# Issuing the gate matrices' stores from ScalarE's queue, one batch behind their eviction, instead of from the sync engine's queue

## The reference, cut to what matters

```python
def peer(xn, w_q, sub_keys, u_tab, v_tab):
    q = (xt @ w_q).reshape(T, PEER_HEADS, 2, PEER_HALF)
    s = jnp.einsum('thpc,hpnc->thpn', q, sub_keys)
    s_top, i_top = lax.top_k(s, PEER_TOPK)
    cand_s = s_top[:, :, 0, :, None] + s_top[:, :, 1, None, :]
    cand_i = i_top[:, :, 0, :, None] * N_KEYS + i_top[:, :, 1, None, :]
    best_s, pos = lax.top_k(cand_s.reshape(...), PEER_TOPK)
    gate = jax.nn.softmax(best_s)
    ...
        act = gelu(jnp.einsum('tkd,td->tk', u_tab[ib], xb))
        return jnp.einsum('tk,tkd->td', act * gb, v_tab[ib])
```

## Time and profile before

| | us |
|---|---|
| median of 3 runs | 1511.92 |
| lowest and highest run | 1506.97 and 1512.82 |
| the profiled execution, its time | 1506.98 |
| its span in the trace | 1505.2 |
| TensorE, VectorE, ScalarE, GpSimd busy over the span | 1447.5, 1245.2, 828.0, 506.6 |
| mean granted TensorE clock, share of full speed | 0.99 |

### The profile page before, as it was taken

How to read it: one execution, slowest core, us unless ns; L and a number is a source line. 1 busy time by engine, 2 the same in 40 slices (tenths; PEclk the granted TensorE clock), 3 DMA queues, 4 the chain that set the end, 5 groups by cost and what they waited for, 6 DMA issues and landing times.

```text
span 1505.2 us, 25263 instructions
## 1 busy us (share of the span) xinstructions
PE 1447.5 (96%) x9438; PEld 1307.3 (87%) x9438; DVE 1245.2 (83%) x2383; ACT 828.0 (55%) x1571; POOL 506.6 (34%) x425
## 2 busy tenths in 40 slices
PE   6999789999999999999989989999999999999999
PEld 6898678779999999999989879999888888878787
DVE  4638778674799799899669849999999989998997
ACT  4453454133244677778768644444566555555653
POOL 4111530010078877777621103323222212221210
PEclk9999899999999999999999999999999999999999
DMA  5230001421158799999899999998999999999993
GB/s 190 89 102 1 8 30 34 166 98 71 51 194 276 272 334 351 360 346 333 301 375 392 394 334 356 392 376 325 398 410 411 412 408 410 411 408 411 403 405 133
DMA packets 168871, 420.49 MB, mean 279 GB/s; under 512 B 12944, under 2 KB 100144, under 8 KB 152240
## 3 DMA queue, kind: packets, MB, share of 16 engines
q1 hardware_dynamic: 126064, 234.06, 42.8%
q0 software_dynamic: 27712, 167.82, 28.3%
q10 hardware_dynamic: 14976, 17.05, 3.1%
HBM read 372.44 MB, written 46.40 MB: 278 GB/s over the span
## 4 chain that ended last, share of the span: by engine, by line
PE 41%; DMA 15%; DVE 12%; issue 4%; ACT 2%; POOL 1%; SPq 0%; ACTq 0%; DVEq 0%
DMA v_raw<-in_peer_v 9%; PE bank L2105 6%; PE bank L2100 6%; PE bank L2101 6%; DMA gates<-gate_stage 4%; PE bank L2122 4%; PE bank L2431 3%; PE bank L2433 3%; PE bank L2432 3%; DVE v_lo L2507 3%; PE bank L2419 2%; PE bank L2420 2%; PE bank L2421 2%; DVE v_lo_late L2507 2%; DVE pair_sum L1822 1%
## 5 line engine op out<-in xcount | busy, mean ns | idle before, releaser
L2100 PE MATMUL bank<-x_hi,u_split 128*128 128x320 f32 x832 | 252.9, 316 | 3.6 <-ACT u_split L2160 3.6
L2101 PE MATMUL bank<-x_lo,u_split 128*128 128x320 f32 x832 | 246.4, 309 | 0.0
L1798 POOL DMA_INDIRECT scores<-in_peer_uv,pair_index x86 | 106.5, 1239 | 379.5 <-DVE pair_sum L1822 375.4
L2478 ACT ACTIVATE act_tile<-onehots 128x384 f32<-128x384 f32 x128 | 124.2, 970 | 74.2 <-DVE act_lo L2520 71.5
L2100 PEld LDWEIGHTS bank<-x_hi,u_split 128*128 128x128 f32 x832 | 157.1, 189 | 4.6 <-issue 4.6
L2101 PEld LDWEIGHTS bank<-x_lo,u_split 128*128 128x128 f32 x832 | 156.8, 188 | 0.0
L2105 PE MATMUL bank<-x_hi,u_split 128*128 128x320 f32 x832 | 139.6, 309 | 0.7 <-POOL u_split L2003 0.7
L2003 POOL TENSOR_TENSOR u_split<-u_raw,u_split 128x1024 fp32r<-128x1024 f32 x41 | 99.4, 2426 | 91.5 <-DVE u_split L2003 58.2
L2105 PEld LDWEIGHTS bank<-x_hi,u_split 128*128 128x128 f32 x832 | 127.1, 189 | 0.9 <-POOL u_split L2003 0.9
L2431 PE MATMUL bank<-v_hi,act_hi 128*128 128x512 f32 x304 | 120.0, 395 | 3.0 <-DVE v_lo L2507 2.9
L2433 PE MATMUL bank<-v_hi,act_lo 128*128 128x512 f32 x304 | 119.1, 392 | 0.0
(11 more groups left out here) (434 smaller groups left out, 4022.2 us busy)
## 6 DMA issues: line engine op xcount, KB each, us to landing
v_raw<-in_peer_v SPq DMA_DIRECT2D x128, 512.0 KB, 11.2
u_raw<-in_peer_u SPq DMA_DIRECT2D x64, 512.0 KB, 5.6
u_raw_more<-in_peer_u SPq DMA_DIRECT2D x64, 512.0 KB, 5.8
gates<-gate_stage SPq DMA_DIRECT2D x24, 1024.0 KB, 13.4
onehots<-gates SPq DMA_DIRECT2D x32, 768.0 KB, 11.9
early_gelus<-early_gelu ACTq DMA_DIRECT2D x104, 160.0 KB, 5.5
gelu_tile<-early_gelus SPq DMA_DIRECT2D x104, 160.0 KB, 11.2
w_raw<-in_w_in SPq DMA_DIRECT2D x9, 1024.0 KB, 5.0
```

The source lines that it names most:

```text
L1798: pool.indirect_dma_start(self.slot(k), None, self.table, bass.IndirectOffsetOnAxis(ap=self.sidx[:, k:k + 1], axis=0)).then_inc(self.lande ...
L2100: nc.tensor.matmul(out, uh[:, q, w], m.xh[:, k, P + NS:], start=(k == 0), stop=False)
L2101: nc.tensor.matmul(out, uh[:, q, w], m.xl[:, k, P + NS:], start=False, stop=False)
L2478: nc.scalar.activation(af[n % 2][:], gt[:, it % 2, :, jj], ACT.Copy).then_inc(gate_cols, 1)
```

## The change

`store_gates` moves from SP's program into ScalarE's. ScalarE calls it in every odd turn n from 3 on, right behind `evict(n - 1, 0)`, for batch n - 2, whose second eviction was made in the turn before; the last store (batch 47) comes behind the loop. What is stored, its size, its pieces, the two halves of `stage` and the semaphores stay as they were. In the changed kernel ScalarE's lines stand about ten lower in number (L2150 for 2160, L2163 for 2173, L2182 for L2192), and the store is L2191.

```diff
@@ SP
-                def store_gates(n):
-                    b, k = BATCHES[n]
-                    q = n // 2 % 2
-                    banks.wait_taken(sp, ("G", b, k, BT // 4 - 1))
-                    t0 = (b - 1) * P + (k + 1) * BT - ST
-                    sp.dma_start(gates[:, :, t0:t0 + ST, :].rearrange("g i t j -> i g (t j)"),
-                                 stage[:, q].rearrange("p g t j -> p g (t j)")).then_inc(stored[q], 16)
...
                 for n in range(NB_):
                     for t in ups_of[n + AHEAD_U] if n + AHEAD_U < NB_ else []:
                         load_u(t + NU)
-                    if n % 2:
-                        store_gates(n)
@@ ScalarE
+                def store_gates(n):
+                    b, k = BATCHES[n]
+                    q = n // 2 % 2
+                    banks.wait_taken(act, ("G", b, k, BT // 4 - 1))
+                    t0 = (b - 1) * P + (k + 1) * BT - ST
+                    act.dma_start(gates[:, :, t0:t0 + ST, :].rearrange("g i t j -> i g (t j)"),
+                                 stage[:, q].rearrange("p g t j -> p g (t j)")).then_inc(stored[q], 16)
...
                             for t in ups_of[n - 1][i:i + 1]:
                                 gelu(t)
                             evict(n - 1, i)
+                            if i == 0 and n >= 2 and n % 2 == 1:
+                                store_gates(n - 2)
...
                     if n == LAST_DOT + 1:
                         up_rows.gelu(act)
+                store_gates(NB_ - 1)
                 for n in range(EARLY - LAST, EARLY):
                     gelu(n)
```

## The result

| | before | after |
|---|---|---|
| median, us | 1511.08 | 1531.88 |
| lowest and highest of four runs | 1506.97 and 1512.82 | 1527.6 and 1534.04 |
| the profiled execution, its time | 1506.98 | 1533.86 |
| its span | 1505.2 | 1532.0 |

The ratio is 1.0132, with a 95% interval from 1.0114 to 1.015: the change costs 20.8 us. The forecast was 1515 us, 3 us slower, with a range to 1525. The sign is right and the size isn't.

What follows compares the result with a forecast made beforehand. TensorE bounds routing until 758 us, then ScalarE's waits for stores of gates show one for one. Loop +7, burst -2, end -2 make +3 on the 1511.9 median: 1515 us, 8 in 10 between 1505 and 1525.

Steps and rivals of the forecast that it cites:

- The loop of the late part: Six pairs of late batches, E(34) to E(46): each pair waits for a whole store landing, 78.9 us against 71.9, +7 us.
- the lag: Late part: the store of gates goes out an eviction later, 3.3 us later than SP issued it, leaving at most one under way.
- E(36): E(n) is the first eviction of batch n, here batch 36; it began at 796.34 us in the kernel before.
- The queue behind the store: ScalarE's gelu store behind a store of gates: held about 1.3 us early (price 0), 2.7 us late (nothing added).
- L: Landing time of a store of gates: median 11.0 us early, 16.1 late; forecast to fall to 12.0 to 13.2 late.
- slower, in the early part: Rival, early part: hold, issue and buffers' wait exceed 2.7 us, TensorE runs dry; +10 us, 1522 us, chance 0.07.
- The burst: Gathers at 758 us: store of batch 29 goes out 2 us earlier, the next later; -2 us, between -4 and +2.
- The end of routing: After store of batch 47: u tile 103's load is freed, gelu stores wait behind the store; -2 us, between -5 and +3.
- ScalarE held in its issues: Rival, late part: ScalarE's first gelu store held behind each store of gates; +10 us, 1522 us (1528 at worst), chance 0.21.
- the faster direction: Rival: on its own queue the store lands sooner, under 10.9 us late; -9 us, about 1503 us, chance 0.15.

Runs made afterwards that it cites:

- The run meant to isolate the gain: The kernel before, with SP issuing the load of u tile 103 ahead of the last store of gates and the last load of v behind it: 1510.9 us against 1511.3.

## Why the prediction was wrong

- **The loop of the late part, +7 us: right in its number, in part by luck.** Measured +8.0: 80.0 us for the six pairs (78.9 forecast), with landings of 10.9 to 15.7 us by the evictions that they released. The mean is right, the single pairs spread more (11.0 to 15.7 us, forecast 12.6 to 13.7), and the first of them (11.5 us) didn't end on a store. What I took for its cause, the lag, is only half of it: on SP's queue the same lag costs 3.8 us in these pairs. With the same closed loop they took 75.8, 80.0 or 85.9 us, by what else stood in the queues, and without it 87.4. (The store of batch 35 went out 2.7 us before E(36), not 2.5 as I wrote; the sum doesn't use it.)
- **"The queue behind the store", price 0 in the early part: failed, +7.9 us.** The hold itself was seen in the earlier trace rows, with the share of L at which it ends. The step that failed is its size: 1.3 us came from SP's hold at 4.7 us behind a store with L = 11, and a gelu's store 3.4 us behind, and the one of 629.82 us was held 8.02, until 11.06 us behind the store. The trace gives that store a landing of 16.6 us (matched by order), so the share, 0.67, is near the 0.53 to 0.65 that I had read, and L is what was too small. The absorbed 2.7 us were exceeded once in full, and TensorE ran dry for 4.2 us at a stretch. What I had put at nothing without a word is the clock: it fell to 0.50 in that wait and cost about 2.5 us more. Moving the gelu's stores away brings E(30) back to 751 us: shown. The rival "slower, in the early part" had the place right, but gave it many small sums where there was mainly one large hold, and got 0.07.
- **"The burst", -2 us: failed, +5.7 us.** I reasoned by bytes: an earlier store is an earlier landing. That held for the store of batch 29: E(30) to E(32) fell from 21.0 to 16.3 us. For the next one I had counted that it goes out only with E(32), and still put it there by the time of before. Before, the store of batch 31 took as long, 23.09 us, but it went out 10 us ahead of E(32). Now it went out with E(32) and still took 23.5 us, so E(32) to E(34) grew from 13.2 to 23.6. In the same late place on SP's queue it took 12.6 us, with 8 KB pieces 11.3: shown. With the gelus gone too it takes 27 to 28 us.
- **"The end of routing", -2 us: failed, +2.4 us.** The same holds (4.41 and 3.81 us) and a wait of 6.30 us for a gelu's store stand in the rows of ScalarE above. The load of the u tile is free as forecast: ScalarE's wait of 7.9 us for it is gone. I had counted 5.1 us from E(46) to the store of batch 47 and 18.9 us from there to the last gelu. Measured are 9.2 and 19.1 us. The step that failed is the first: the gelu's store behind the store of batch 45 had no price, and was held 4.41 us. With the gelus' stores on SP's queue this part takes 22.2 and 23.3 us, against 26.0 before. The run meant to isolate the gain (0.9997) brought the tile no earlier.
- **The remaining 2.8 us.** The first gelu of the next stage is 25.3 us late (914.99 against 889.68), so about 1.4 of them lie ahead of it. There TensorE, which had stood still for 6.0 us, starts at a granted clock of 0.50 (909 to 913 us; 1.00 in the same place before), and 4 us at half the clock are about 2 us. The other 1.5 stay unexplained.
- **The rivals.** "ScalarE held in its issues" gave 1522 us, or 1528 with the larger hold, and had 0.21. Its time is the nearest, its place isn't: it put the cost in the late pairs (92.4 us at worst, measured 80.0), whereas the holds that cost were in the early part and at the end.
- **The error behind all of them** is the one L. I took it as a function of the rate alone, and credited the move to a queue of its own with 0.7 us. I had written that no row showed large DMAs on both hardware queues, and held this open in the faster direction only. The Trainium skill ("DMA: Bandwidth & Descriptors", section "Queues, rings and completion order") says that each DMA engine takes turns between its rings packet by packet; I weighed that as a help for the store. The runs agree with turns, against the store: 13.4 us beside loads instead of 5.8 in front of them, for pieces that need the engines for 3.5 us. That turns between small and large pieces are the reason is the likeliest reading, and the piece sizes bear it out (23.1 us at 512 bytes, 6.8 at 8 KB), but no trace shows a single turn or how many pieces go in one.

## What to carry to other kernels

Before a DMA in small pieces moves to a queue of its own, look at what stood *behind* it: those transfers now run beside it, and if their pieces are large it lands two to four times later (13.4 or 23.1 us for 5.8 or 6.0). Make the pieces larger first; then the choice of queue matters little (2.4 us here, where it was 20.8). And a compute engine should not issue any DMA shortly behind such a one, since the issue itself can hold it for a third to two thirds of the transfer, with all its compute behind it. When such a hold makes TensorE wait, count the clock too: after a wait of 4.2 us it ran 6 us at half speed.

## What was not expected of the hardware

- One store of 1 MB in pieces of 512 bytes lands after 5.1 us alone and 23.1 us beside loads in the other hardware queue and gathers, issued together with the loads and just before the gathers; loads alone make it 13.4 (12.7 with the queues swapped). Standing behind the loads, in their queue, it lands after 21.0.
- An issue behind such a store is held 7.1 to 9.3 us with nothing else on the engine, and up to 10.05 us in the kernel. With 8 KB pieces no issue of ScalarE between 520 and 910 us was longer than 0.9 us.
- With 8 KB pieces the kernel before is 0.5% faster (0.995), more than any place of the store gave here. The gates then lie in another order, which the next stage's loads would have to follow; that wasn't tried.
